# Halved weight splits, three output steps moved later, constants in two transfers, and a cache turned in two row groups

## The reference

```python
def layer(x, pos, s_ret, s_gla, conv_prev, ...):
    n = rmsnorm(x, ln1)
    rq, rk, rv, rg, gq, gk, gv, gg, ga, m_r, m_g = split_cols(n @ w_in)
    ...                                             # rotary on rq, rk
    o_r, s_ret_new = chunked_gated_linear(rq, rk, rv, log_g, s_ret)
    y_r = (group_rmsnorm(o_r, g_ret) * jax.nn.silu(rg)) @ w_ret_out
    z = ga @ w_gate_up + b_gate_up
    log_a = jax.nn.log_sigmoid(z) / GLA_GATE_TAU
    o_g, s_gla_new = chunked_gated_linear(gq, gk, gv, log_a, s_gla)
    y_g = (group_rmsnorm(o_g, g_gla) * jax.nn.silu(gg)) @ w_gla_out
    h = x + (sigmoid(m_r) * y_r + sigmoid(m_g) * y_g) @ w_o
    up = rmsnorm(h, ln2) @ w_up
    uc, conv_tail = causal_dwconv(up[..., :D_FF], conv_prev, conv_w, conv_b)
    return h + (gelu(uc) * up[..., D_FF:]) @ w_down, s_ret_new, s_gla_new, conv_tail
```

## Time and profile before

| | |
|---|---|
| device time, median of 3 runs | 823.83 us (823.05 to 824.13) |
| the profiled execution | 824.17 us, of which its span 822.4 us |
| PE busy | 812.3 us, 99% of the span |
| DVE busy | 588.8 us, 72% |
| ACT busy | 377.9 us, 46% |
| POOL busy | 218.4 us, 27% |
| granted TensorE clock, mean | 0.996 of full speed |

### The profile page before, as it was taken

How to read it: one execution, slowest core, us unless ns; L and a number is a source line. 1 busy time by engine, 2 the same in 40 slices (tenths; PEclk the granted TensorE clock), 3 DMA queues, 4 the chain that set the end, 5 groups by cost and what they waited for, 6 DMA issues and landing times.

```text
span 822.4 us, 15722 instructions
## 1 busy us (share of the span) xinstructions
PE 812.3 (99%) x6522; PEld 798.8 (97%) x6522; DVE 588.8 (72%) x766; ACT 377.9 (46%) x535; POOL 218.4 (27%) x261
## 2 busy tenths in 40 slices
PE   9999999999999999999999999999999999999996
PEld 9989999999989999999999999999999999999996
DVE  5475669487899786766568877777777756778973
ACT  5653244322456363443244544443444424544574
POOL 4028247343427300000530333333322222000020
PEclk9999999999999999999999999999999999999998
DMA  9769968983328963537996686576677873765622
GB/s 272 220 206 173 270 215 182 202 263 103 110 80 149 231 234 97 186 130 231 199 271 195 142 259 202 150 203 202 241 184 202 231 172 103 202 181 172 175 60 108
DMA packets 163090, 152.32 MB, mean 185 GB/s; under 512 B 6710, under 2 KB 144682, under 8 KB 163005
## 3 DMA queue, kind: packets, MB, share of 16 engines
q1 hardware_dynamic: 129420, 109.73, 42.6%
q0 software_dynamic: 33440, 41.09, 26.6%
q10 hardware_dynamic: 160, 0.53, 0.2%
HBM read 145.36 MB, written 58.40 MB: 248 GB/s over the span
## 4 chain that ended last, share of the span: by engine, by line
PE 95%; DVE 3%; issue 1%; ACT 0%; DVEq 0%
PE mm L2063 52%; PE ax L2371 14%; PE mm L2485 8%; PE ax L2485 6%; PE ax L2084 6%; PE mm L2371 4%; PE ax L2089 2%; PE mm L2146 1%; PE mm L2084 1%; DVE grs L1478 1%; DVE wlo L1468 1%; DVE ysil L1725 0%; DVE ylo L1730 0%; DVE wlo L1742 0%; ACT whi L1030 0%
## 5 line engine op out<-in xcount | busy, mean ns | idle before, releaser
L2063 PE MATMUL mm<-nhi,whi 128*128 128x272 f32 x928 | 196.4, 293 | 0.5 <-DVE wlo L1468 0.5
L2063 PE MATMUL mm<-nhi,wlo 128*128 128x272 f32 x928 | 191.9, 288 | 0.0
L2063 PE MATMUL mm<-nlo,whi 128*128 128x272 f32 x928 | 191.4, 288 | 0.0
L1030 ACT ACTIVATE whi<-raw 128x1024 fp32r<-128x1024 f32 (+2 forms) x111 | 128.2, 1190 | 64.8 <-PE mm L2063 34.7
L2063 PEld LDWEIGHTS mm<-nhi,whi 128*128 128x128 f32 x928 | 146.3, 188 | 3.3 <-DVE wlo L1468 1.0
L2063 PEld LDWEIGHTS mm<-nlo,whi 128*128 128x128 f32 x928 | 145.8, 188 | 0.0
L2063 PEld LDWEIGHTS mm<-nhi,wlo 128*128 128x128 f32 x928 | 145.1, 189 | 0.0
L1742 DVE TENSOR_TENSOR wlo<-raw,whi 128x1024 fp32r<-128x1024 f32 (+1 forms) x78 | 84.4, 1124 | 6.6 <-ACT whi L1030 4.1
L1468 DVE TENSOR_TENSOR wlo<-raw,whi 128x2048 fp32r<-128x2048 f32 x27 | 65.2, 2415 | 13.6 <-ACT whi L1030 13.6
L961 POOL DMA_DIRECT2D v_sums<-in_w_up x24 | 30.8, 4230 | 117.4 <-DVE mlo L1813 116.7
L1030 ACT ACTIVATE whi<-ring 128x1408 fp32r<-128x1408 f32 x25 | 34.6, 1384 | 44.0 <-PE ax L2485 24.0
(11 more groups left out here) (393 smaller groups left out, 1975.2 us busy)
## 6 DMA issues: line engine op xcount, KB each, us to landing
raw<-in_w_in SPq DMA_DIRECT2D x36, 512.0 KB, 4.9
raw<-in_w_up SPq DMA_DIRECT2D x36, 512.0 KB, 6.9
ring<-w_sums SPq DMA_DIRECT2D x16, 704.0 KB, 4.8
w_sums<-in_w_down SPq DMA_DIRECT2D x9, 768.0 KB, 10.6
w_sums<-in_w_down POOLq DMA_DIRECT2D x9, 768.0 KB, 9.6
ring<-in_w_down SPq DMA_DIRECT2D x9, 704.0 KB, 4.7
v_sums<-in_w_up SPq DMA_DIRECT2D x24, 256.0 KB, 7.7
v_sums<-in_w_up POOLq DMA_DIRECT2D x24, 256.0 KB, 14.5
```

What stands on the lines that cost most here:

```text
L1030: return act.activation(out, in_, func, **kw).then_inc(done, 1)
L2063: ins = pe.matmul(mm[:, 2 * j + a, 0:HALF], w, x[:, kx, HALF * a:HALF * (a + 1)], start=first and n == 0 and m == 0, stop=last and n == le ...
```

## The change

Four edits. (1) `split` of unit 3 is done as unit 1's was: ACT in two instructions of four row blocks each, DVE in two, the first of which starts when ACT's first is done. (2) The steps `y2 2`, `y2 3` and `y1 4` leave their place behind half 0 of unit 14 and stand inside half 1, behind `ro 3` and ahead of `ri 2`. (3) `c1` comes in two transfers: the identity first in the queue, the ones and eps behind unit 0's weights; PE waits for the second ahead of `rstd1`. (4) The cache is loaded as two blocks of 1408 columns by two transfers, to partitions 0 to 15 and 64 to 79. PE turns them alternately from these two row groups into two PSUM banks, and ACT copies out of both banks with one instruction.

```diff
+IN_HALVES = (1, 3)
...
-        (14, 0): [("y2", 2), ("y2", 3), ("y1", 4)],
...
-        (14, 1): {1: [("rs", 3)], 2: [("rp", 3)], 4: [("rn", 2), ("ro", 3), ("ri", 2)], 6: [...]},
+        (14, 1): {1: [("rs", 3)], 2: [("rp", 3)], 4: [("rn", 2), ("ro", 3), ("y2", 2), ("y2", 3), ("y1", 4), ("ri", 2)], 6: [...]},
...
-    cache = at("cache", [2 * DEC_BATCH, D_FF], C + (NJ + 1) * D_MODEL * 4)
+    cache = at("cache", [GLA_DK + 2 * DEC_BATCH, D_FF // 2], C + (NJ + 1) * D_MODEL * 4)
...
+    CACHE_ROWS = (slice(0, 2 * DEC_BATCH), slice(GLA_DK, GLA_DK + 2 * DEC_BATCH))
...
-        sp.dma_start(c1[:, :], A["c1"]).then_inc(c1_in, 16)
+        sp.dma_start(c1[:, 0:C1_ONE], A["c1"][:, 0:C1_ONE]).then_inc(c1_in, 16)
...
+        sp.dma_start(c1[:, C1_ONE:C1_N], A["c1"][:, C1_ONE:C1_N]).then_inc(ones_in, 16)
...
-        pool.dma_start(cache[:, :], A["cache_conv"][0].rearrange("b r d -> (b r) d")).then_inc(cache_in, 16)
+        for r in range(2):
+            pool.dma_start(cache[CACHE_ROWS[r], :], A["cache_conv"][0].rearrange("b r d -> (b r) d")[:, D_FF // 2 * r:D_FF // 2 * (r + 1)]
+                           ).then_inc(cache_in, 16)
...
-            if s == ("split", 1):
-                act.wait_ge(landed[1], 32)
-                run(whi[1][:, 0:4, :], raw[1][:, 0:4, :], ACT.Copy, hi1_part)
+            if k == "split" and s[1] in IN_HALVES:
+                u = s[1]
+                act.wait_ge(landed[1], 32 * (u // 2 + 1))
+                if u >= 2:
+                    act.wait_ge(filled[1], fills(1, u - 2))
+                run(whi[1][:, 0:4, :], raw[1][:, 0:4, :], ACT.Copy, half_high)
                 run(whi[1][:, 4:8, :], raw[1][:, 4:8, :], ACT.Copy, hi_ready)
...
-                run(pt[:, :, 2:18], bank("cache", 0)[:, 0:16 * KF].rearrange("p (f r) -> p f r", r=16), ACT.Copy,
-                    drained_sem("cache"))
+                b = 2 * (USE["cache"] % 2)
+                run(pt[:, :, 2:18].rearrange("p (b f) r -> p b f r", b=2),
+                    ax[:, b:b + 2, 0:16 * KH].rearrange("p b (f r) -> p b f r", r=16), ACT.Copy, drained_sem("cache"))
...
-            if s == ("split", 1):
-                dve.wait_ge(hi1_part, 1)
+            if k == "split" and s[1] in IN_HALVES:
+                u = s[1]
+                dve.wait_ge(half_high, IN_HALVES.index(u) + 1)
                 st.did(dve.tensor_tensor(wlo[1][:, 0:4, :], raw[1][:, 0:4, :], whi[1][:, 0:4, :].bitcast(F32), ALU.subtract))
-                dve.wait_ge(hi_ready, 2)
+                dve.wait_ge(hi_ready, u + 1)
...
-                pe.wait_ge(cache_in, 16)
+                pe.wait_ge(cache_in, 32)
                 aux_take(pe, "cache")
-                for t in range(KF):
-                    turn(bank("cache", 0)[:, 16 * t:16 * (t + 1)], cache[:, P * t:P * (t + 1)],
-                         filled_sem("cache") if t == KF - 1 else None)
+                for t in range(KH):
+                    for b, r in enumerate(CACHE_ROWS):
+                        ins = pe.transpose(bank("cache", b)[:, 16 * t:16 * (t + 1)], cache[r, P * t:P * (t + 1)], ident[r, r])
+                ins.then_inc(filled_sem("cache"), 1)
             elif k == "rstd1":
                 pe.wait_ge(acc1_done, 1)
+                pe.wait_ge(ones_in, 16)
```

More of the change, by code:

```diff
@@ L409, in build @@
     zeros_ready = sem("zeros_ready")
-    c1_in, c2_in, vec_in, cache_in, rope_in, wg_in = map(sem, ("c1_in", "c2_in", "vec_in", "cache_in", "rope_in", "wg_in"))
+    c1_in, ones_in, c2_in, vec_in, cache_in, rope_in, wg_in = map(sem, ("c1_in", "ones_in", "c2_in", "vec_in", "cache_in", "rope_in", "wg_in"))
     x_in = [sem(f"x_in{j}") for j in range(NJ + 1)]
@@ L415, in build @@
     hi0_part, lo0_part = sem("hi0_part"), sem("lo0_part")
-    hi1_part = sem("hi1_part")
+    half_high = sem("half_high")
     filled = [sem(f"filled{j}") for j in range(2)]
```

## The result

The changed kernel takes 825.95 us in the median of its 22 executions, the kernel before 823.53 us in executions on the same chip. Two of the 22 took 985 us at a mean granted clock of 0.751; they stand in that median (825.65 us without them) and not in the ratio. The ratio of the changed kernel to the kernel before is **1.0024, with a 95% interval of 1.0018 to 1.0031**: 2.0 us slower, 1.5 to 2.6. The forecast was 825.2 us, with a range of 823.6 to 826.6. The time lies in the range, and the way it went, a wait for the first gate in place of the wait for `rss`, is the one forecast. The size was not put together rightly: the lateness was smaller than forecast, and rival (c), the clock, came on top of it. The two errors, 0.45 us too much and 1.60 us too little, have opposite signs, so it is in part luck that the time lies in the range.

What follows compares the result with a forecast made beforehand. PE, busy 99% of the span, was taken as the bound. Start 0, unit 3 and cache -0.09 and moved steps +1.44 gave +1.35 us on the 823.83 median: 825.2 us, range 823.6 to 826.6.

Steps and rivals of the forecast that it cites:

- rival (c): At unit 16: the clock falls in the new 2.2 us wait, costing another 1.7 us, 826.9 us; chance 0.09.
- Constants, 0 us: At the start: constants landing earlier meet a PE still running its zeros, so splitting their transfer gains 0.
- The sign that was named for it: At the start: PE's timeline up to 37 us should be unchanged to 0.1 us.
- Cache turns: Before unit 3: 22 turns from two row groups take 0.76 us, half of 1.53; far ends 1.53 and 2.6 us.
- Unit 3 in halves, 0.09 us: At unit 3: PE could start 0.77 us sooner, but 0.68 becomes waiting ahead of `za`; 0.09 us gained.
- The step that named `ga`: At `za`: PE's wait labelled "issue" is really for DVE's `ga`, ending 47.14; `za` would start at 47.15.
- the slack at unit 3: At unit 3: PE would have to be 1.2 us later than planned to miss `za` at 47.15.
- Rival (b): At `za`: the wait has another cause than `ga`, so halves and cache turns pay in full, 824.5 us; chance 0.06.
- The gain on offer at rn 2, 0.72 us: At `rn 2`: moving three steps ends `rss` earlier, so PE no longer waits for it; 0.72 us on offer.
- DVE's reciprocal, 2.15 us late: Ahead of `ri 2`: DVE's moved steps wait for ACT's late `yhi` copies; reciprocal at 247.8 against 245.63, 2.15 us later.
- Lateness at unit 16: At unit 16, half 0: `gsig` ends 1.44 us later, making a new PE wait of 2.2 us; 1.44 us lost.
- Rival (a): Before the first gate: DVE makes up its lateness, so the move simply removes a wait, 823.0 us; chance 0.10.

Runs made afterwards that it cites:

- cache_only: Kernel before with only the cache turns in two row groups; 776.98 us from the sums of rstd1 to the last sums of squares, against 776.97; not timed.
- early_copies: Changed kernel with ACT's two copies to yhi left at their old place, only DVE's three instructions moved; ratio to the kernel before 0.9986 (0.9978 to 0.9995).
- move_only: Kernel before with only the three output steps moved; ratio to the kernel before 1.0030 (1.0020 to 1.0041).

## Why the prediction came out as it did

- **Constants, 0 us.** Right as far as it can be measured: 776.97 us from the mark either way, ratio 0.9998. The sign that was named for it, TensorE's start up to 37 unchanged to 0.1 us, was not kept, as the mark came 0.30 us sooner; but two programs with the same start differ there by 2.26 us (37.22 and 34.96), so the sign could tell nothing.
- **Cache turns.** Forecast 0.76 us, half of 1.53; they took 0.85 (39 ns each, 70 before). The forecast that nothing of this reaches the end was right: cache_only changed 0.01 us.
- **Unit 3 in halves, 0.09 us.** Right: 0.10 alone, 0.09 with the cache turns. The step that named `ga`, where the row says "issue", held; `za` starts 46.87 - 36.92 = 9.95 us behind the mark, 10.02 before. Two slips in the working changed nothing: by its own rows the slack at unit 3 is 47.15 - 4.77 - 41.45 = 0.93 us, not 1.2 (4.77 is the time from the start of unit 3 to the place of `za`), and the wait at `za` 0.25 + 0.68 = 0.93, not 0.8; 0.97 was measured. Rival (b) is refuted. The Trainium skill ("Perfetto Trace Analysis", "Optimizing Scalar/DVE Operations") says that breaking up instructions "may allow work to be completed sooner". This case's trace agrees for the work that was broken up: unit 3 starts 0.78 us sooner behind the mark (4.22 against 5.00). For the whole program it gave 0.10 us of the 0.77 by itself. More came only when what stood behind was moved or shortened as well: 0.73 us with `za` a block later, 0.43 with the table loaded early, 0.28 with TensorE's wait in halves. How much of these three needs the halves was not run.
- **The gain on offer at rn 2, 0.72 us.** The wait went, and more than forecast: `rn 2` starts 205.49 us behind the mark, 206.47 before, which is 0.98 sooner, 0.09 of it from unit 3. The profile counts idle time from the end that it gives the last product, but back to back the next pair starts 0.16 us ahead of that end (a row of two products is 0.41 us long, and such rows start every 0.25 us). So this stop cost its 0.72 us of idle time and that overlap, and the term was taken too small.
- **DVE's reciprocal, 2.15 us late.** The step that was mis-sized. It started 1.73 us later (210.14 against 208.41 from the mark). ACT's root came 0.3 us sooner than forecast, for the reason just given and unit 3, and the first `yhi` starts 0.10 us ahead of the end of `rso`. Then 0.74 us were absorbed on the way to `gsig` where 0.71 was forecast: it starts 227.31 us behind the mark, 226.32 before. **Lateness at unit 16: 0.99 us, forecast 1.44.** The new wait is 1.88 us long, forecast 2.2.
- **Rival (c), chance 0.09.** It happened in the profiled execution and, by the mean clock, in 18 of 20. Its price, worked out as 1.7 us, is close to the 1.60 measured, but partly by luck: the 3.5 us at half pace were taken from the loads at the start, where the record of the granted clock shows no fall (last section). Its chance was too low for what was known. It rested on the one stop in the middle of the program, 0.72 us, that had no effect, and the forecast wait was three times that, longer than anything the trace showed to be harmless. The rows gave no chance for such a length; with one near even, the forecast would have stood between 825.2 and 826.9.
- **Rival (a).** Refuted for the change as it is: DVE did not make up its lateness. early_copies shows what it would have looked like, and how little was missing.

The sum: forecast -0.09 + 1.44 = +1.35 us; measured from the mark -0.09 + 0.99 + 1.60 = +2.50 us in the profiled execution, and 2.0 (1.5 to 2.6) by the ratio. Two of 20 executions without the fall explain 0.16 us of that difference; the rest is within the interval. As for the chances, 0.72 stood on a time within 0.2% of the kernel before and 0.25 on slower; measured are 0.24%, between 0.18 and 0.31, so the likelier of the two was probably missed, if narrowly.

## What to carry to other kernels

A step in an order that all engines walk is several instructions on several engines: before it is moved, look on each of them at what it will queue behind, and move only the part that is in the way. Where a wait of TensorE is taken away, the next wait behind it is the bound, so follow its chain (here `ga`, the reciprocal, the root, a table load) before the gain is counted. A new stop of TensorE that is longer than any in the trace is to be priced twice, for its length and for the clock behind it.

## What the runs showed of the hardware

**The pace of the start is not in the granted clock.** The granted clock of the first 12 us reads 1.00 in the profiles, before and after. Yet the same loads of zeros and inputs run at two paces, some 215 to 232 ns and some 108 to 121 ns each, and the moment of the change differs between profiles of programs that start alike. In the changed kernel's profile and in move_only's, the loads ahead of the first unit:

```profile
6.65 1.72 PEld L2098 LDWEIGHTS ax<-c,x_nat 128*128 128x128 f32 x8
8.36 1.76 PEld L2093 LDWEIGHTS mm<-zeros 128*128 128x128 f32 x8
10.04 0.91 PEld L2098 LDWEIGHTS ax<-c,x_nat 128*128 128x128 f32 x8
```

```profile
5.75 0.86 PEld L2088 LDWEIGHTS ax<-c,x_nat 128*128 128x128 f32 x8
6.57 0.97 PEld L2083 LDWEIGHTS mm<-zeros 128*128 128x128 f32 x8
8.12 0.86 PEld L2088 LDWEIGHTS ax<-c,x_nat 128*128 128x128 f32 x8 [0.58 <-DMA x_nat<-in_x_prompt]
```

In the first, 8 loads take 1.72 us until about 10 us; in the second they take 0.86 us already from 5.75 on, and TensorE then waits for the inputs instead. Both profiles with the early change and with the late one occur with and without the split of the constants. The start of `ax<-acc,c` ranges over 2.6 us in the profiles, about as much as the executions of the kernel before differ among themselves (821.9 to 824.2 us). A comparison of two single profiles must therefore start behind it. What decides the moment was not tried.

**The lower level does not begin at the stop.** In the changed kernel the stop of 1.88 us ends at 265.09, the granted clock is 1.00 until 266.0 and 0.51 in the half microsecond after that. In move_only a stop of the same length ends at 263.21, and the granted clock is 0.56 already from 263.5 to 264.0, so the fall comes some 0.9 us behind the one stop and 0.3 us behind the other. In both the clock is back at 1.00 some 3 us after the fall. The loss from the mark is nearly the same, 2.50 and 2.57 us.
